# Weight tiles moved in pairs, 8 KB in a row for each partition, with twelve ring slots in place of ten and half the descriptor scratch

## The chip, the cores and the metric

The kernel runs on one core of one Trainium2 chip. The metric is the device time of one execution in microseconds, given as the median of several. Five engines work side by side: TensorE (PE; matrix products), VectorE (DVE), ScalarE (ACT), GpSimd (POOL) and SyncE (SP), which here only issues transfers. The core's 16 DMA engines serve the transfers of all of them. Everything is float32 except the one-hot factors.

## The reference

A two-layer decoder trunk over 272 tokens (16 meta tokens and 256 real ones) of width 1024. Layer 0 mixes tokens by latent attention, layer 1 by a gated linear recurrence; each is followed by the same kind of expert layer, which is what matters here:

```python
q = (xb @ w_query).reshape(-1, PEER_HEADS, 2, PEER_QHALF)
s = jnp.einsum('thpd,pkd->thpk', q, sub_keys)
sv, si = lax.top_k(s, PEER_TOPK)
...
eidx = jnp.take_along_axis(cidx, top_p, axis=-1)   # 16 experts of 16384 for each token and head
g = jax.nn.softmax(top_s, axis=-1)
act = jax.nn.gelu(jnp.einsum('thkd,td->thk', u_tab[eidx], xb))
return jnp.einsum('thk,thkd->td', g * act, v_tab[eidx])
```

So every token meets 128 experts (8 heads of 16), each one row of 4 KB in `u_tab` and one in `v_tab`, tables of 16384 rows (64 MB each per layer).

## The kernel before, in words

**The stream of tiles.** All weights pass through one ring in on-chip memory, `raw`, of `SLOTS` = 10 slots of 128 partitions by 4 KB (512 KB). `tiles_in_order` lists the 593 tiles of the whole program: 25 of the attention layer, 272 of the expert layer (16 query tiles, 128 of `u`, 128 of `v`), 24 of the recurrence, and 272 again. `Tiles.fetch` (L227 to L232), run by SyncE, issues one transfer for each tile; tile g waits until TensorE has finished tile g - 10 (the semaphore `done` counts two halves for each tile). TensorE waits for `landed` of the slot (L254) in `multiply_raw` (L259 to L271) for query and u tiles and in `apply_v` (L1161 to L1167) for v tiles. `fetch` of one stage reaches `SLOTS` tiles into the next, ahead of that stage's own small loads. `wait_halves` lets other engines wait for a place in the stream.

**The expert layer.** Its tokens are treated in two ways. For 160 of them (TD) the layer is computed densely: TensorE multiplies each u tile with all 160 tokens, ScalarE applies gelu (L1225) into `act_w`, VectorE multiplies in the gates, and TensorE applies each v tile to the result, collecting in PSUM. A float32 product appears as two matmul records, so a tile of 8 products is 16 records at L267 (queries, u) or L1159 (v). The gates are spread out by products of one-hot factors that VectorE builds in groups of 8 tokens (L1135 to L1142): 20 groups for each half of the experts, TensorE's part at L1122, 24 records for each group; they stand between the last 40 u tiles and between the first 40 v tiles, one for each two tiles. Before them TensorE waits, after u tile 84, for VectorE's `placed` (its products are at L1477).

The other tokens (112 in layer 0, 96 in layer 1) are done by gathering. GpSimd (L1179 to L1186) issues one indirect transfer for each set of 128 rows of 4 KB (512 KB, as much as a tile), into one of `NBUF` = 8 buffers: 112 of `u_rows` and then 112 of `v_rows` in layer 0, 96 and 96 in layer 1, 416 in all. It waits for the indices (`rows_found`) and for VectorE to have taken the row set 8 places earlier (`rows_taken`). VectorE takes a set of u rows with a product and sum (`dot`, L1316 to L1323) and a set of v rows with a multiply and add (`add_row`, L1330 to L1340). Where it does so is written out by hand: 6 sets after each pair of searches for the top 16 (L1357), 9 and 9 about the spreading of the gates (L1370, L1383), 2 with each group of one-hot factors (L1396), and the rest, 78 sets in layer 0 and 56 in layer 1, one by one, paced by the v tiles from 40 to 118 (L1400 to L1404).

**The end of the layer.** Before v tiles 112, 116, 120 and 124 (112, 116 and 124 in layer 1) TensorE folds in one copy of the gathered sums (L1492 to L1505, 16 records at L1501). Fold b waits until `rows_taken` has 32 (b + 1) sets of v rows; the last one waits for all of them.

**Memory.** The kernel's tensors nearly fill the on-chip memory; a part at its start, 16 KB for each partition by default, is kept for the descriptors of GpSimd's transfers (L1681).

Of the kernel before, what the change touches and what calls it, by code (L numbers as in the profile page):

```python
# [20 lines left out]
P = 128  # L21
D = 1024
DC = D // P
# [12 lines left out]
PH, NK, TOPK, QH = 8, 128, 16, 128  # L36
# [1 line left out]
HALF = NK // 2  # L38
ST = 8
PARTS = 3  # L40
SLOTS = 10
LEAD = 2
HW = D // 2

# [56 lines left out]
class Steps:  # L101


    def __init__(self, eng, sem):
        self.eng, self.sem, self.n = eng, sem, 0
# [109 lines left out]
class Tiles:  # L215

    def __init__(self, ctx, mem, tiles):
        self.mem, self.tiles = mem, tiles
        self.landed = [ctx.sem(f"landed{k}") for k in range(SLOTS)]
        self.done = ctx.sem("tiles_done")

    def fetch(self, sp, first, last):  # L227

        for g in range(first, min(last, len(self.tiles))):
            if g >= SLOTS:  # L230
                sp.wait_ge(self.done, 2 * (g - SLOTS + 1))
            sp.dma_start(self.mem.raw[:, g % SLOTS, :], self.tiles[g]).then_inc(self.landed[g % SLOTS], 16)  # L232


class Stream:
# [14 lines left out]
            pe.sem_inc(free, 1)  # L250

    def wait_landed(self, pe, n):
        g = self.base + n
        pe.wait_ge(self.mem.tiles.landed[g % SLOTS], 16 * (g // SLOTS + 1))  # L254

    def tile(self, n):
        return self.mem.raw[:, (self.base + n) % SLOTS, :]

    def multiply_raw(self, pe, n, out, x, scaled=None):  # L259

# [1292 lines left out]
def tiles_in_order(d):  # L1553

    def layer(n):
        v_tiles = d[f"v_rows{n}"].rearrange("(i p) f -> i p f", p=P)
        return ([d["query"][n][k] for k in range(2 * PH)] + [d["u"][n][k] for k in range(NK)]
                + [v_tiles[k] for k in range(NK)])

    mixed = [[d["mla_down"][k] for k in range(MLA_TILES - DC)] + [d["mla_out"][k] for k in range(DC)],  # L1560
             [d["lru_w"][k] for k in range(LRU_TILES)]]
    return mixed[0] + layer(0) + mixed[1] + layer(1)


# [62 lines left out]
def lay_out(inputs):  # L1627

    a = {k: np.asarray(v) for k, v in inputs.items()}
    chunked = lambda t: np.ascontiguousarray(t.T.reshape(DC, P, -1).transpose(1, 0, 2))  # L1630
    columns = lambda v: v.reshape(-1, P).T
    half = ROPE // 2
    swap = np.r_[half:ROPE, 0:half]

    w_in = a["mla_w_in"][0]
    lat, kr = w_in[:, :QLORA + KVLORA], w_in[:, QLORA + KVLORA:]
    q_up = a["mla_w_q_up"][0].reshape(QLORA, HEADS, NOPE + ROPE)
    q_rope = q_up[:, :, NOPE:]
    q_up = np.concatenate([x.reshape(QLORA, -1) for x in (q_rope, q_rope[:, :, swap], q_up[:, :, :NOPE])], axis=1)
    kv_up = a["mla_w_kv_up"][0].reshape(KVLORA, HEADS, NOPE + VH)  # L1640

    def half_tiles(w):
        w = w.reshape(-1, P, w.shape[1] // P, P).transpose(2, 0, 1, 3).reshape(-1, 4, P, P)
        return w.transpose(0, 2, 1, 3).reshape(-1, P, HW)

    k_up, v_up = kv_up[:, :, :NOPE].reshape(KVLORA, -1), kv_up[:, :, NOPE:].reshape(KVC, P, 2, HW)
    up = np.concatenate([half_tiles(q_up), half_tiles(k_up), v_up.transpose(2, 0, 1, 3).reshape(-1, P, HW)])
    up = up.reshape(-1, 2, P, HW).transpose(0, 2, 1, 3).reshape(-1, P, D)
    down = column_tiles(np.concatenate([lat, kr, kr, kr[:, swap], kr[:, swap]], axis=1))
    vec = [a["mixer_norm"][0], a["mixer_norm"][1], a["ffn_norm"][0], a["ffn_norm"][1], a["final_norm"],  # L1650
           a["lru_b_gate_a"][0], a["lru_b_gate_x"][0], a["lru_conv_b"][0], *a["lru_conv_w"][0], a["lru_lambda"][0],
           a["mla_q_norm"][0], a["mla_kv_norm"][0]]
    con, idm = constants()
    layers = a["peer_u"].shape[0]
    lru_in = a["lru_w_in"][0]
    u = a["peer_u"].reshape(layers, NK, NK, DC, P).transpose(0, 1, 4, 3, 2)
    return {
        "x": chunked(a["x"][0]),
        "meta": chunked(a["meta_tokens"]),
        "pos": np.ascontiguousarray(a["positions"]),  # L1660
        "con": con,
        "idm": idm,
        "vec": np.ascontiguousarray(np.concatenate([columns(v) for v in vec], axis=1)),
        "mla_down": np.concatenate([down, up]),
        "mla_out": column_tiles(a["mla_w_out"][0]),
        "query": column_tiles(a["peer_w_query"]),
        "keys": np.ascontiguousarray(a["peer_sub_keys"].transpose(0, 3, 1, 2)),
        "u": np.ascontiguousarray(u).reshape(layers, NK, P, D),
        **{f"u_rows{n}": np.ascontiguousarray(a["peer_u"][n]) for n in range(layers)},
        **{f"v_rows{n}": np.ascontiguousarray(a["peer_v"][n]) for n in range(layers)},  # L1670
        "lru_w": np.concatenate([column_tiles(w) for w in (lru_in[:, D:], lru_in[:, :D], a["lru_w_out"][0])]),
        "lru_wa": np.ascontiguousarray(a["lru_w_gate_a"][0].transpose(1, 0, 2)),
        "lru_wx": np.ascontiguousarray(a["lru_w_gate_x"][0].transpose(1, 0, 2)),
    }
# [16 lines left out]
```

## Time and profile before

| | |
|---|---|
| median of 3 runs | 1613.38 us (1613.03 to 1615.23) |
| the profiled execution | 1615.82 us |
| its span in the trace | 1613.8 us |
| TensorE busy | 1582.1 us (98%) |
| VectorE busy | 1101.5 us (68%) |
| GpSimd busy | 494.1 us (31%) |
| moved by DMA | 534.94 MB, mean 331 GB/s |
| SyncE's queue, packets and share of the 16 DMA engines | 89938, 50.7% |
| GpSimd's queue | 59904, 34.5% |

The rows below come from the trace of the profiled execution; their times count from the start of its span. A share of DMA above 1.00 means that packets of an engine overlap. In the list of stretches each engine's busy time stands with its number of instructions in brackets; in the chain and in the instruction lists a row begins with its start and its length. "<-" names what ended the idle time before an instruction.

### The profile page before, as it was taken

To read this page: it belongs to the slowest core of one execution; us is meant where nothing else is said; L and a number is where in the kernel's file an instruction comes from. 1 tells how busy PE (TensorE), PEld (TensorE's weight loads), DVE (VectorE), ACT (ScalarE), POOL (GpSimd) and SP (SyncE) were. 2 spreads that over 40 slices of the span, in tenths; PEclk is the share of its full clock that TensorE was granted. 3 is DMA by queue.
4 is the path that set the end of the run, shared out by engine and by line. 5 is a ranking of instruction groups with operands and counts; after the bars stand their busy time and mean duration, and the time that the engine had idled before them with its cause. 6 is when DMAs were issued, how large, how long until landed. Compare 5 with 4: busy or idle time off the path is not lost.

```text
span 1613.8 us, 30119 instructions
## 1 busy us (share of the span) xinstructions
PE 1582.1 (98%) x12128; PEld 1506.9 (93%) x12128; DVE 1101.5 (68%) x2478; ACT 209.5 (13%) x604; POOL 494.1 (31%) x423
## 2 busy tenths in 40 slices
PE   9999999999899999999999999999999999999997
PEld 7688899999899999998898888999999999999997
DVE  3373379998899998545537425999879989944441
ACT  2251221111011000000003312111211100000000
POOL 0000033335444456533300001333534435533310
PEclk9999999999999999999999999999999999999999
DMA  6304489999999999999984446999999999999991
GB/s 245 131 16 147 137 304 389 384 394 406 409 408 409 401 409 408 409 409 409 409 326 155 144 149 227 339 397 386 396 409 408 408 405 408 408 410 408 409 378 60
DMA packets 149979, 534.94 MB, mean 331 GB/s; under 512 B 17617, under 2 KB 20434, under 8 KB 149842
## 3 DMA queue, kind: packets, MB, share of 16 engines
q1 hardware_dynamic: 89938, 314.90, 50.7%
q0 software_dynamic: 59904, 218.13, 34.5%
q8 instruction: 96, 1.57, 0.4%
q14 instruction: 41, 0.34, 0.1%
HBM read 531.92 MB, written 1.05 MB: 330 GB/s over the span
## 4 chain that ended last, share of the span: by engine, by line
PE 79%; DVE 10%; DMA 8%; issue 3%; ACT 0%; DVEq 0%; SPq 0%; ACTq 0%; POOLq 0%
PE ps L267 37%; PE ps L1159 30%; DMA raw<-in_v_rows 6%; PE ps L1122 4%; DVE big L1322 3%; PE ps L728 2%; PE ps L279 2%; DMA big<-in_u_rows,big 2%; DVE big L1272 1%; PE ps L1501 1%; PE ps L738 1%; DVE big L1268 1%; PE ps L1433 1%; DVE big L1298 1%; DVE big L1300 1%
## 5 line engine op out<-in xcount | busy, mean ns | idle before, releaser
L267 PE MATMUL ps<-big,raw 128*128 128x160 f32 (+2 forms) x5104 | 798.5, 318 | 2.5 <-ACT big L1225 2.5
L267 PEld LDWEIGHTS ps<-big,raw 128*128 128x128 f32 x5104 | 751.5, 191 | 35.6 <-issue 3.1
L1159 PE MATMUL ps<-big,raw 128*128 128x160 f32 x4096 | 579.1, 301 | 6.5 <-DVE big L1154 2.3
L1159 PEld LDWEIGHTS ps<-big,raw 128*128 128x128 f32 x4096 | 559.6, 190 | 15.7 <-DMA raw<-in_v_rows 12.7
L1185 POOL DMA_INDIRECT big<-in_u_rows,big x208 | 250.3, 1203 | 733.4 <-DVE big L1308 376.5
L1339 DVE SCALAR_TENSOR_TENSOR big<-big 128x1024 f32<-128x1024 f32 x201 | 258.0, 1284 | 191.3 <-PE ps L1159 107.7
L1185 POOL DMA_INDIRECT big<-in_v_rows,big x208 | 240.5, 1156 | 320.6 <-DVE big L1339 255.1
L1322 DVE CUSTOM_DVE_ANT_0 big<-big 128x1024 f32<-128x1024 f32 x208 | 244.4, 1222 | 22.4 <-DMA big<-in_u_rows,big 19.8
L1225 ACT ACTIVATE big<-ps 128x160 f32<-128x160 f32 x256 | 77.4, 303 | 512.7 <-PE ps L267 474.0
L374 ACT ACTIVATE big<-h 128x272 f32<-128x272 f32 (+1 forms) x32 | 12.7, 419 | 645.8 <-DVE h L1414 597.3
L1268 DVE MAX8 big<-big 128x8 f32<-128x128 f32 (+1 forms) x99 | 33.5, 339 | 88.3 <-ACT big L1194 76.3
L1142 DVE TENSOR_TENSOR i_gate<-i_hot,g 128x512 bf16<-128x512 bf16 x240 | 87.2, 419 | 0.0
L1122 PEld LDWEIGHTS ps<-i_gate,j_hot 128*128 128x128 bf16 x1920 | 69.3, 98 | 7.9 <-DVE i_gate L1142 4.9
L1122 PE MATMUL ps<-i_gate,j_hot 128*128 128x64 bf16 x1920 | 71.6, 193 | 4.6 <-DVE i_gate L1142 4.6
L1154 DVE TENSOR_TENSOR big<-big,ps 128x512 f32<-128x512 f32 x80 | 54.8, 685 | 24.5 <-PE ps L1122 21.4
L1138 DVE TENSOR_TENSOR j_hot<-iota,idx 128x1024 bf16<-128x1024 bf16 x80 | 54.8, 685 | 0.0
L789 DVE TENSOR_TENSOR h<-h,ps 128x272 f32<-128x272 f32 (+1 forms) x16 | 6.9, 429 | 44.2 <-PE ps L267 44.2
L1135 DVE TENSOR_TENSOR i_hot<-iota,idx 128x512 bf16<-128x512 bf16 x80 | 33.5, 419 | 0.1
L279 PE MATMUL ps<-big,raw 128*128 128x272 f32 (+1 forms) x128 | 30.3, 390 | 2.4 <-DVE big L577 2.4
L1272 DVE FIND_INDEX8 big<-big 128x8 uint32<-128x128 f32 (+1 forms) x99 | 31.1, 333 | 0.0
L1271 DVE FIND_INDEX8 big<-big 128x8 uint32<-128x128 f32 (+1 forms) x99 | 31.1, 332 | 0.0
L279 PEld LDWEIGHTS ps<-big,raw 128*128 128x128 f32 x128 | 24.2, 190 | 7.2 <-DMA raw<-in_mla_down 2.7
(173 smaller groups left out, 762.7 us busy)
## 6 DMA issues: line engine op xcount, KB each, us to landing
raw<-in_u SPq DMA_DIRECT2D x256, 512.0 KB
raw<-in_v_rows SPq DMA_DIRECT2D x256, 512.0 KB
raw<-in_query SPq DMA_DIRECT2D x32, 512.0 KB
raw<-in_lru_w SPq DMA_DIRECT2D x24, 512.0 KB
raw<-in_mla_down SPq DMA_DIRECT2D x17, 512.0 KB
raw<-in_mla_out SPq DMA_DIRECT2D x8, 512.0 KB
big<-in_u_rows,big POOLq DMA_INDIRECT x208
big<-in_v_rows,big POOLq DMA_INDIRECT x208
```

Of the source, the lines that this page charges most:

```text
L267: mm = pe.matmul(out, w[:, c * P:(c + 1) * P], x[:, c, :], start=(c == 0), stop=(c == DC - 1))
L279: mm = pe.matmul(self.bank(n), self.tile(n)[:, c * P:(c + 1) * P], x[:, c, :], start=(c == 0), stop=(c == DC - 1), skip_group_check=True)
L1122: mm = pe.matmul(o, mem.j_hot[:, t // 2, :, t % 2], mem.i_gate[:, k, t // 2, :, t % 2], start=(k == 0), stop=(k == PARTS - 1))
L1138: step.add(dve.tensor_tensor(mem.j_hot[:, :, :, :], mem.iota[:, :, :].unsqueeze(1).to_broadcast(wide), pairs(mem.idx[:, 1, tok], wide), AL ...
L1142: ins = dve.tensor_tensor(mem.i_gate[:, k], mem.i_hot[:, :, :, :], pairs(mem.g[:, k, tok], wide_i), ALU.mult)
L1154: dve.tensor_tensor(w, w, g, ALU.mult).then_inc(gated, 1)
L1159: return pe.matmul(accumulator(c), w, act_w[:, i, :], start=start, stop=False, skip_group_check=True)
L1185: pool.indirect_dma_start(bufs[:, b, :], None, (u_rows if n < ROWS else v_rows)[:, :], bass.IndirectOffsetOnAxis(rows_at[:, k:k + 1], 0)). ...
L1225: act.activation(act_w[:, i:i + 1, :], mem.ps[:, i % 2, 0:TD].unsqueeze(1), ACT.Gelu_apprx_tanh).then_inc(st.free[i % 2], 1)
L1268: for k, op in enumerate((lambda v, spare, f, at: dve.max(f[:, 0:8], v), lambda v, spare, f, at: dve.match_replace(spare, f[:, 0:8], v, NE ...
L1322: dve.tensor_tensor_reduce(buf, buf, reps[:, copy_of(n), :], 1.0, 0.0, ALU.mult, ALU.add, dots[:, n:n + 1]).then_inc(rows_taken, 1)
L1339: dve.scalar_tensor_tensor(rep, bufs[:, n % NBUF, :], w, rep, ALU.mult, ALU.add).then_inc(rows_taken, 1)
```

## The change

Query, u and v tiles are laid out in device memory in pairs, so that each partition's part of two tiles lies in 8 KB on end, and one transfer moves both into two neighbouring slots. The tiles of attention and recurrence stay single. The ring has 12 slots. A transfer is issued once both its slots are free. The v tiles now come from an array of their own, laid out in pairs, and no longer from the one that the gathers read. The scratch for the descriptors of GpSimd's transfers goes from 16 KB to 8 KB for each partition.

```diff
-SLOTS = 10
+SLOTS = 12
...
-    def __init__(self, ctx, mem, tiles):
-        self.mem, self.tiles = mem, tiles
+    def __init__(self, ctx, mem, transfers):
+        self.mem, self.transfers = mem, transfers
         self.landed = [ctx.sem(f"landed{k}") for k in range(SLOTS)]
         self.done = ctx.sem("tiles_done")
+        self.sem_of, self.count, self.total, used = [], [], 0, [0] * SLOTS
+        for count, _ in transfers:
+            k = self.slot(self.total)
+            assert k + count <= SLOTS
+            used[k] = used[k] + 16
+            self.sem_of = self.sem_of + [self.landed[k]] * count
+            self.count = self.count + [used[k]] * count
+            self.total = self.total + count
+
+    def slot(self, g):
+        return (g + 1) % SLOTS
+
+    def wait_landed(self, pe, g):
+        pe.wait_ge(self.sem_of[g], self.count[g])
 
     def fetch(self, sp, first, last):
 
-        for g in range(first, min(last, len(self.tiles))):
-            if g >= SLOTS:
-                sp.wait_ge(self.done, 2 * (g - SLOTS + 1))
-            sp.dma_start(self.mem.raw[:, g % SLOTS, :], self.tiles[g]).then_inc(self.landed[g % SLOTS], 16)
+        g = 0
+        for count, tiles in self.transfers:
+            if first <= g < last:
+                k = self.slot(g)
+                if g + count > SLOTS:
+                    sp.wait_ge(self.done, 2 * (g + count - SLOTS))
+                sp.dma_start(self.mem.raw[:, k:k + count, :], tiles).then_inc(self.landed[k], 16)
+            g = g + count
...
     def layer(n):
-        v_tiles = d[f"v_rows{n}"].rearrange("(i p) f -> i p f", p=P)
-        return ([d["query"][n][k] for k in range(2 * PH)] + [d["u"][n][k] for k in range(NK)]
-                + [v_tiles[k] for k in range(NK)])
+        return ([(2, d["query"][n][k]) for k in range(PH)] + [(2, d["u"][n][k]) for k in range(NK // 2)]
+                + [(2, d["v"][n][k]) for k in range(NK // 2)])
...
+    def by_two(tiles):
+        tiles = tiles.reshape(layers, -1, 2, P, D).transpose(0, 1, 3, 2, 4)
+        return np.ascontiguousarray(tiles)
...
-        "query": column_tiles(a["peer_w_query"]),
+        "query": by_two(column_tiles(a["peer_w_query"])),
...
-        "u": np.ascontiguousarray(u).reshape(layers, NK, P, D),
+        "u": by_two(u),
+        "v": by_two(a["peer_v"]),
...
-    nc = bacc.Bacc("TRN2", target_bir_lowering=False, num_devices=1)
+    nc = bacc.Bacc("TRN2", target_bir_lowering=False, num_devices=1, dynamic_dma_scratch_size=8192)
```

## Rows read from the trace of the kernel before

**Rows 1.** The page: TensorE, the packets, and the two queues that carry nearly all.
```profile
PE 1582.1 (98%) x12128; PEld 1506.9 (93%) x12128; DVE 1101.5 (68%) x2478; ACT 209.5 (13%) x604; POOL 494.1 (31%) x423
...
DMA packets 149979, 534.94 MB, mean 331 GB/s; under 512 B 17617, under 2 KB 20434, under 8 KB 149842
...
q1 hardware_dynamic: 89938, 314.90, 50.7%
q0 software_dynamic: 59904, 218.13, 34.5%
```

**Rows 2.** Busy time by stretches; last columns: TensorE's clock, DMA share, GB/s.
```profile
0.00:25.00 25.00, 21.21 (x101) 16.53 (x102) 11.52 (x33) 6.62 (x9) 3.27 (x7) 1.00 0.87 315
...
375.00:825.00 450.00, 436.13 (x3883) 425.39 (x3882) 332.12 (x507) 20.14 (x61) 201.53 (x173) 0.99 1.03 408
...
600.00:625.00 25.00, 25.00 (x276) 24.81 (x276) 24.48 (x39) 0.00 (x0) 12.94 (x10) 1.00 1.03 408
...
700.00:725.00 25.00, 24.31 (x169) 22.84 (x168) 11.37 (x10) 0.00 (x0) 8.43 (x9) 1.00 1.03 409
725.00:750.00 25.00, 23.77 (x158) 21.35 (x157) 12.55 (x10) 0.00 (x0) 9.37 (x10) 1.00 1.03 409
750.00:775.00 25.00, 23.82 (x158) 21.40 (x157) 12.26 (x11) 0.00 (x0) 9.33 (x10) 1.00 1.03 409
775.00:800.00 25.00, 23.85 (x162) 21.68 (x160) 12.11 (x10) 0.00 (x0) 8.86 (x10) 1.00 1.03 409
...
1404.00:1560.00 156.00, 156.00 (x1158) 156.00 (x1154) 67.43 (x54) 0.00 (x0) 49.10 (x50) 1.00 1.03 409
```

**Rows 3.** The chain of waits in order of time, v tiles of layer 0; end of layer 1.
```profile
629.46 69.64 PE ps L1159 x512
...
774.03 23.17 DMA raw<-in_v_rows
797.24 2.44 PE ps L1159 x16
799.68 1.70 PE ps L1501 x16
...
820.64 1.70 PE ps L1501 x16
...
831.12 1.69 PE ps L1501 x16
...
1590.52 1.70 PE ps L1501 x16
```

**Rows 4.** VectorE's instructions in order of time, rows of V taken in layer 0.
```profile
660.57 1.28 DVE L1339 SCALAR_TENSOR_TENSOR big<-big 128x1024 f32<-128x1024 f32 x1 [1.26 <-DMA big<-in_v_rows,big]
663.13 1.28 DVE L1339 SCALAR_TENSOR_TENSOR big<-big 128x1024 f32<-128x1024 f32 x1 [1.28 <-DMA big<-in_v_rows,big]
...
823.18 1.28 DVE L1339 SCALAR_TENSOR_TENSOR big<-big 128x1024 f32<-128x1024 f32 x1 [1.27 <-DMA big<-in_v_rows,big]
```

**Rows 5.** VectorE and TensorE in order of time, before the one-hot products of layer 0.
```profile
419.59 1.23 DVE L1322 CUSTOM_DVE_ANT_0 big<-big 128x1024 f32<-128x1024 f32 x1 [1.32 <-DMA big<-in_u_rows,big]
...
404.93 1.41 PE L1477 MATMUL ps<-token,big 128*128 128x16 bf16 x50 [1.20 <-DVE big L1379]
...
424.11 1.46 PE L1122 MATMUL ps<-i_gate,j_hot 128*128 128x64 bf16 x24 [4.63 <-DVE i_gate L1142]
```

**Rows 6.** The same of layer 1, and the last row that it takes.
```profile
1191.25 1.23 DVE L1322 CUSTOM_DVE_ANT_0 big<-big 128x1024 f32<-128x1024 f32 x1 [1.33 <-DMA big<-in_u_rows,big]
...
1194.63 1.09 DVE L1142 TENSOR_TENSOR i_gate<-i_hot,g 128x512 bf16<-128x512 bf16 x3
...
1201.30 0.89 PE L1122 MATMUL ps<-i_gate,j_hot 128*128 128x64 bf16 x24
...
1571.39 1.28 DVE L1339 SCALAR_TENSOR_TENSOR big<-big 128x1024 f32<-128x1024 f32 x1 [0.89 <-PE ps L1159]
```

**Rows 7.** GpSimd's gathers of V: nanoseconds of one (shortest, median, longest).
```profile
L1185 POOL DMA_INDIRECT big<-in_v_rows,big x208: 932/940/1876, 524.7 to 1547.8; - x104
```

More of the change, by code:

```diff
@@ L252, in wait_landed @@
     def wait_landed(self, pe, n):
-        g = self.base + n
-        pe.wait_ge(self.mem.tiles.landed[g % SLOTS], 16 * (g // SLOTS + 1))
+        self.mem.tiles.wait_landed(pe, self.base + n)
     def tile(self, n):
-        return self.mem.raw[:, (self.base + n) % SLOTS, :]
+        return self.mem.raw[:, self.mem.tiles.slot(self.base + n), :]
     def multiply_raw(self, pe, n, out, x, scaled=None):
@@ L1555, in layer, with single @@
     def layer(n):
-        v_tiles = d[f"v_rows{n}"].rearrange("(i p) f -> i p f", p=P)
-        return ([d["query"][n][k] for k in range(2 * PH)] + [d["u"][n][k] for k in range(NK)]
-                + [v_tiles[k] for k in range(NK)])
-    mixed = [[d["mla_down"][k] for k in range(MLA_TILES - DC)] + [d["mla_out"][k] for k in range(DC)],
-             [d["lru_w"][k] for k in range(LRU_TILES)]]
+        return ([(2, d["query"][n][k]) for k in range(PH)] + [(2, d["u"][n][k]) for k in range(NK // 2)]
+                + [(2, d["v"][n][k]) for k in range(NK // 2)])
+    def single(tile):
+        return 1, tile.unsqueeze(1)
+    mixed = [[single(d["mla_down"][k]) for k in range(MLA_TILES - DC)] + [single(d["mla_out"][k]) for k in range(DC)],
+             [single(d["lru_w"][k]) for k in range(LRU_TILES)]]
     return mixed[0] + layer(0) + mixed[1] + layer(1)
@@ L1655, in lay_out @@
     lru_in = a["lru_w_in"][0]
-    u = a["peer_u"].reshape(layers, NK, NK, DC, P).transpose(0, 1, 4, 3, 2)
+    u = a["peer_u"].reshape(layers, NK, NK, DC, P).transpose(0, 1, 4, 3, 2).reshape(layers, NK, P, D)
+    def by_two(tiles):
+        tiles = tiles.reshape(layers, -1, 2, P, D).transpose(0, 1, 3, 2, 4)
+        return np.ascontiguousarray(tiles)
     return {
```

## The prediction

> **What bounds the kernel now.** I read the page first, then the busy time by stretches, then the chain of waits, then the instruction lists of the two expert stages. The page shows TensorE busy for 98% of the span, and two DMA queues sharing the 16 DMA engines: SyncE's, which streams the 512 KB tiles, and GpSimd's, which gathers 512 KB of table rows at a time; together about 85% of the engines' time [rows 1]. The stretches show where the second number matters. From 375 to 825 us, in layer 0, the engines are full: share 1.03, 408 GB/s [rows 2]. So one 512 KB transfer costs 524,288 B / 409 GB/s = 1.28 us of the DMA engines, whichever queue it is from, and in this stretch any transfer that comes earlier pushes another one back by 1.28 us.
>
> TensorE needs less than that. From 629.46 us 512 matmul records, 32 tiles of 16 records, take 69.64 us: 2.176 us a tile [rows 3], or 241 GB/s. But with both queues loaded each gets every other turn: the vector engine's row steps come 2.56 us apart behind the gathers [rows 4], exactly 2 x 1.28, which leaves the tile stream one tile in 2.56 us too. TensorE eats the tiles that had been fetched ahead, and from about 700 us starves. Four stretches of 25 us hold 169, 158, 158 and 162 records where 25 / 2.176 x 16 = 184 would fit [rows 2]; the chain of waits has the tile transfers in it there, the last until 797.24 us [rows 3]. The missing 89 records are 12 us.
>
> The end of the stage is set by a second condition. Before V tiles 112, 116, 120 and 124 TensorE folds in the gathered rows (the 16-record pieces at 799.68, 820.64 and 831.12), each fold waiting for 32 more rows to be taken, the last one for all 224. The last row had landed at 823.18 and was taken at 824.46 [rows 4]; the last fold began at 831.12 [rows 3]. So today the gathers end 6.7 us before they are needed, and the tiles are what is late. Both draw on the same DMA time: the tiles are late, the gathers have 6.7 us in hand.
>
> **The change part by part.** *Rows of 8 KB in each transfer.* Both queues now move 4 KB rows: nearly all packets lie between 2 and 8 KB, and the 593 tile transfers are 144 packets each, as are the 416 gathers [rows 1]. Equal packets and equal shares: that fits engines which take a packet from each queue in turn. It would fit turns by bytes as well, and the trace can't tell the two apart. I take turns by packet. The tile queue then moves 8 KB for each 4 KB of a gather and can have 2/3 of 409 = 273 GB/s, above the 241 it needs. The ring of tiles stays full and TensorE doesn't starve.
>
> The Trainium skill ("DMA: Bandwidth & Descriptors", "Queues, rings and completion order") says that each DMA engine goes round its queues a packet at a time. By that rule it is the change of packet that moves the shares, and the rule speaks against this change; with turns by bytes in its place the result is the first rival's.
>
> Gain for TensorE: from 629.46, 72 tiles up to V tile 112 at 2.176 us are 156.7, so fold 0 at 786.1 in place of 799.7; then 10.48 us for each fold with its four tiles (831.12 - 820.64), so it stands before fold 3 at 817.6 in place of 831.1: 13.5 us sooner [rows 3].
>
> Price for the gathers: what is fetched sooner for TensorE is taken from them, and the last gather is found by counting transfers. Tile 111 had landed by 797.24 [rows 3], and at one in 2.56 us ten more by 823.2: 122 V tiles. After the change TensorE is held before tile 124 with a full ring, and twelve slots mean that tiles 124 to 135 (the last eight already those of the recurrent layer) have landed: 136. These 14 extra transfers come before the last gather: 14 x 1.28 = 17.9 us, so it lands at 841.1, is taken 1.3 us later, and fold 3 begins at 842.4, **11.3 us later** than now. The 13.5 us are gained and then waited away: TensorE stands idle some 25 us at folds 2 and 3. Nothing gives that back: the full ring goes into a stage that is not short of DMA.
>
> *Rate of the longer rows.* No row shows 8 KB packets. Lowest end: no gain, since at a share of 1.03 the packets already overlap. Highest end: the first 25 us, where part of the packets are 1 KB, move 315 GB/s at share 0.87, or 362 at share 1, against 409/1.03 = 397 later: 10% [rows 2]. I take 2%, near the low end, as the engines are never without a packet in the stretch that counts. From 375 us to the last gather about 183 tiles land (47 u tiles and 136 of V), so 1% is 183 x 1.28 x 0.01 = 2.3 us, and 2% is 4.7. Fold 3 at 837.7: **+6.6 us**.
>
> The Trainium skill ("Perfetto Trace Analysis", "DMA Optimizations") holds that going from 2 KB to 4 or 8 KB can raise throughput dramatically; the runs so far show nothing from 4 to 8. Its page "DMA: Bandwidth & Descriptors" ("Bandwidth") gives 425 GB/s for a 16 MB transfer; as an estimate that would be 4%, and the sum +2.
>
> *The earlier join in layer 0.* At 380 to 424 us TensorE waits 1.2 us for `placed` and 4.63 us for the first one-hot products, behind rows that land every 2.56 us [rows 5]. With the ring kept full, gathers get 409 - 241 = 168 GB/s, 3.1 us each, while TensorE runs, and all of it while it stands. In those 38 us TensorE takes about 16.3 tiles against 15 landed, so the gathers are set back by 1 to 2 transfers: 0 to 2.5 us. This is inside the 14 counted above, as the DMA engines are full from here to the last gather; alone it would not set the end.
>
> *The stretch with one-hot products* (424 to 629): two tiles and two rows in each 5.15 us are 407 GB/s, and VectorE is busy 24.48 of 25 us [rows 2]. The gathers keep 409 - 204 = 205 GB/s, just their need. Costs nothing, but has no margin.
>
> *Layer 1.* The rows taken just before the products come from the gather of 1191.25, the products begin at 1201.30 [rows 6]: VectorE has the first one-hot tiles ready at 1195.7, which leaves 5.6 us of cover, and the setback there is about 2 to 3 transfers, 2.6 to 3.8 us. The last row is taken by 1572.7, fold 2 comes at 1590.5 [rows 3, 6]; even ten transfers more, 12.8 us, are covered. TensorE is busy 156.0 of 156 us from 1404 to 1560 [rows 2], so nothing is gained either: 0. If that cover were gone, each transfer would cost 1.28.
>
> *Two more slots, pairs, fewer issues.* A pair is issued when both its slots are free and is usable when both tiles are in, but at 12 slots it is asked for no later than 10 tiles ahead of use, which is what a tile has now. SyncE issues half as many transfers; it mostly waits. 0.
>
> *Half the scratch.* A gather is 144 packets on 16 engines, 9 on each, and at most 8 are under way: 72 entries. GpSimd takes 0.94 us for one [rows 7] against 2.56 between them, so even a wait of a microsecond at each wrap hides. Between 0 and 1 us; 0.
>
> Sum: +6.6 us. The profiled execution took 1615.82 us (span 1613.8), 2.4 above the median of 1613.38: 1622.4 in its terms, **1620.0** in those of the median.
>
> **Rivals.** *Shares stay equal* (turns by bytes). For it: the trace fits it as well. The tiles keep one turn in two; two more slots are worth at most 2 x 2.56 = 5.1 us where they could be filled before the drought, and 2% on some 158 tiles gives 4.0. Between 0 and 9 us sooner, the 6.7 us that the gathers have in hand being nearly the cap; taken 4: 1609.4. Chance 0.23.
>
> *The rate decides: faster.* Shares shift, but 8 KB rows run over 4.8% faster; there 4.8 x 2.3 us cancel the 11.3. At 8% fold 3 comes at 842.4 - 18.7 = 823.7, 7.4 sooner: 1606.0; TensorE's own arrival caps it at 13.5. Against it: the share of 1.03. Chance 0.12.
>
> *The change doesn't do what it says*: the hardware cuts 8 KB rows into 4 KB packets again. Then only the slots count: 0 to 5 us sooner, taken 2.5: 1610.9. Chance 0.10.
>
> Forecast: 0.55. Its own range is 1613 (4.6% more rate) to 1627 (no gain, and two tiles miscounted: 11.3 + 2.6).
>
> **Numbers.** The range takes in the first and third rival and the forecast, and leaves out the larger gains of the rate: 1608.0 to 1627.0. A measurement here tells about 0.2%, 3.2 us, from nothing. Faster by more: 0.15 of the first rival, 0.10 of the second, 0.04 of the third: 0.29. Within: 0.16. Slower: 0.55.
>
> **What would show it.** Right: SyncE's queue falls from 89,938 to about 50,800 packets; 700 to 800 us hold some 736 records in place of 647 and no tile transfer stands in the chain; rows there come about 3.1 us apart; TensorE waits at L1501 for VectorE's L1339 some 15 to 25 us in all, and the last fold of layer 0 begins near 838. Wrong: rows still 2.56 us apart (equal shares), over 420 GB/s in the full stretch (the rate), or the last fold before 831.

## The result, and the profile of the changed kernel

Four executions of the changed kernel took 1628.67 us in the median (1625.92 to 1630.10), four of the kernel before 1614.31 (1613.03 to 1615.55). The ratio is **1.0087**, 95% interval 1.0070 to 1.0104: slower by 14 us, where 6.6 was forecast. The profiled execution took 1630.1 us, its span is 1628.0, 14.2 longer than before.

The page of the changed kernel, beside [rows 1]:

```profile
PE 1578.0 (97%) x12128; PEld 1510.6 (93%) x12128; DVE 1102.1 (68%) x2478; ACT 209.5 (13%) x604; POOL 495.4 (30%) x423
...
DMA packets 110810, 534.91 MB, mean 329 GB/s; under 512 B 13266, under 2 KB 16083, under 8 KB 75859
...
q1 hardware_dynamic: 50770, 314.89, 48.9%
q0 software_dynamic: 59904, 218.13, 34.1%
```

SyncE's queue has 39,168 packets fewer. That is 272 pairs x 144: a pair is now 144 packets, as one tile was, 9 on each of the 16 engines. And 4,351 of the packets under 512 B are gone, 16 for each of the 272 pairs (4,352) but for one. So a transfer's ninth packet on each engine is a small one beside eight rows. This will matter below.

Its stretches, with the columns of [rows 2] (last three: TensorE's clock, DMA share, GB/s):

```profile
375.00:825.00 450.00, 432.41 (x3923) 429.77 (x3921) 319.54 (x496) 20.20 (x61) 198.80 (x172) 0.98 1.02 410
600.00:625.00 25.00, 25.00 (x276) 24.81 (x276) 24.48 (x40) 0.00 (x0) 12.67 (x11) 1.00 1.02 406
700.00:725.00 25.00, 25.00 (x186) 25.00 (x185) 10.29 (x9) 0.00 (x0) 7.48 (x8) 1.00 1.02 414
725.00:750.00 25.00, 25.00 (x186) 25.00 (x185) 10.28 (x8) 0.00 (x0) 8.42 (x9) 1.00 1.02 417
...
775.00:800.00 25.00, 25.00 (x192) 25.00 (x191) 12.03 (x10) 0.00 (x0) 10.27 (x10) 1.00 1.02 415
800.00:825.00 25.00, 18.15 (x137) 17.90 (x135) 11.11 (x10) 0.00 (x0) 9.11 (x10) 0.92 1.02 410
825.00:850.00 25.00, 11.92 (x65) 11.79 (x65) 13.77 (x17) 0.58 (x2) 2.29 (x2) 0.60 0.43 159
1404.00:1560.00 156.00, 156.00 (x1205) 155.88 (x1204) 74.98 (x72) 0.00 (x0) 54.91 (x54) 1.00 1.02 415
```

TensorE no longer starves from 700 to 800 us: 186 and 192 records in 25 us where there were 158 to 169. The engines move 415 GB/s there in place of 409. Then comes the price. From 825 to 850 us TensorE works for less than half of the time, at a granted clock of 0.60 (0.50, the lower of its two levels, from 838 to 842 us), while the DMA engines are at 0.43: the ring is full, the last gathers land, and everything waits for VectorE and for one fold. The chain of waits, in order of time, beside [rows 3]:

```profile
785.45 19.62 DMA big<-in_v_rows,big
805.15 1.30 DVE big L1352
...
809.17 17.57 DMA big<-in_v_rows,big
826.82 1.30 DVE big L1352
...
836.74 1.29 DVE big L1352
838.08 3.59 PE ps L1514 x16
841.67 8.34 PE ps L1172 x48
...
1604.78 1.71 PE ps L1514 x16
```

Gathers stand where tiles stood. The fold that began at 831.12 [rows 3] begins at 838.08, and takes 3.59 us where it took 1.69; the 48 records after it take 8.34. In the kernel before the same chain read:

```profile
832.81 6.62 PE ps L1159 x48
...
846.34 6.42 PE ps L279 x28
```

The rows of V that VectorE takes, in order of time, beside [rows 4]; 34 of them between 699.26 and 798.80 us are 3.02 us apart in the mean:

```profile
666.26 1.29 DVE L1352 SCALAR_TENSOR_TENSOR big<-big 128x1024 f32<-128x1024 f32 x1 [0.92 <-DMA big<-in_v_rows,big]
669.41 1.28 DVE L1352 SCALAR_TENSOR_TENSOR big<-big 128x1024 f32<-128x1024 f32 x1 [1.86 <-PE ps L1172]
...
826.82 11.20 DVE L1352 SCALAR_TENSOR_TENSOR big<-big 128x1024 f32<-128x1024 f32 x8 [0.32 <-DMA big<-in_v_rows,big]
```

The last eight come back to back, 1.4 us each: once the ring is full, gathers land at least as fast as VectorE takes them. TensorE in order of time (the last fold, then the two joins), and VectorE's last late row of u in layer 1, beside [rows 5, 6]:

```profile
838.08 3.59 PE L1514 MATMUL ps<-con,big 128*128 128x16 f32 x16 [19.93 <-DVE big L1352]
...
424.86 1.46 PE L1135 MATMUL ps<-i_gate,j_hot 128*128 128x64 bf16 x24 [6.99 <-DVE i_gate L1155]
...
1197.01 1.40 PE L1490 MATMUL ps<-token,big 128*128 128x16 bf16 x50
...
1214.22 1.46 PE L1135 MATMUL ps<-i_gate,j_hot 128*128 128x64 bf16 x24 [2.67 <-DVE i_gate L1155]
...
1209.70 1.23 DVE L1335 CUSTOM_DVE_ANT_0 big<-big 128x1024 f32<-128x1024 f32 x1 [2.21 <-DMA big<-in_u_rows,big]
```

**The ledger of the 14.2 us.** The last fold of layer 0 begins 7.0 us later. The fold and the 48 records behind it take 3.59 + 8.34 in place of 1.69 + 6.62, so 3.6 us go to the clock. Layer 1 loses about 4: there TensorE has a new wait of 2.67 us for the one-hot products and starts them at half clock (1.46 us for 24 records where [rows 6] has 0.89). The sum is 14.6 less some tenths gained elsewhere; after the join nothing more is lost (1604.78 against 1590.52 at the last fold of layer 1 is +14.26). Single places move more than the sum does: the same kernel, executed again for experiment 6, has its last fold of layer 0 at 835.52, its new wait in layer 1 at 3.74 us and the last fold of layer 1 some 13.3 us later than before. So 2.5 us between two profiles at the last fold of layer 0 tell nothing by themselves.

### The profile page after: what moved, and what is told of

Its sections match the earlier page's. It is cut to its first block, busy times and chain, and to the rows that moved or that the text cites. A ratio compares the mean times of both kernels' runs of the same rounds, so it can differ in the third digit from the quotient of the medians.

```text
span 1628.0 us, 29847 instructions
## 1 busy us (share of the span) xinstructions
PE 1578.0 (97%) x12128; PEld 1510.6 (93%) x12128; DVE 1102.1 (68%) x2478; ACT 209.5 (13%) x604; POOL 495.4 (30%) x423
## 3 DMA queue, kind: packets, MB, share of 16 engines
q1 hardware_dynamic: 50770, 314.89, 48.9%
## 4 chain that ended last, share of the span: by engine, by line
PE 52%; DVE 25%; DMA 14%; issue 7%; POOL 1%; ACT 0%; DVEq 0%; another core or an unknown queue 0%; SPq 0%; POOLq 0%; ACTq 0%
PE ps L280 23%; PE ps L1172 18%; DMA big<-in_v_rows,big 10%; DVE big L1335 7%; DMA big<-in_u_rows,big 4%; DVE big L1352 4%; PE ps L1135 3%; PE ps L741 2%; PE ps L292 2%; DVE i_gate L1155 2%; DVE big L1285 1%; DVE big L1281 1%; DVE big L1311 1%; DVE big L1313 1%; DVE big L1167 1%
## 5 line engine op out<-in xcount | busy, mean ns | idle before, releaser
L280 PEld LDWEIGHTS ps<-big,raw 128*128 128x128 f32 x5104 | 752.1, 191 | 35.6 <-issue 3.0
L1172 PE MATMUL ps<-big,raw 128*128 128x160 f32 x4096 | 571.4, 301 | 2.2 <-DVE big L1167 2.2
L1172 PEld LDWEIGHTS ps<-big,raw 128*128 128x128 f32 x4096 | 560.5, 191 | 2.9 <-issue 2.4
L1352 DVE SCALAR_TENSOR_TENSOR big<-big 128x1024 f32<-128x1024 f32 x201 | 258.0, 1283 | 203.5 <-PE ps L1172 109.6
L1514 PE MATMUL ps<-con,big 128*128 128x32 f32 (+1 forms) x112 | 14.8, 286 | 19.9 <-DVE big L1352 19.9
L1514 PEld LDWEIGHTS ps<-con,big 128*128 128x128 f32 x112 | 14.8, 212 | 20.2 <-DVE big L1352 20.2
L1285 DVE FIND_INDEX8 big<-big 128x8 uint32<-128x128 f32 (+1 forms) x99 | 31.1, 330 | 0.0
```

Source lines behind the costliest of these rows:

```text
L280: mm = pe.matmul(out, w[:, c * P:(c + 1) * P], x[:, c, :], start=(c == 0), stop=(c == DC - 1))
L1172: return pe.matmul(accumulator(c), w, act_w[:, i, :], start=start, stop=False, skip_group_check=True)
L1352: dve.scalar_tensor_tensor(rep, bufs[:, n % NBUF, :], w, rep, ALU.mult, ALU.add).then_inc(rows_taken, 1)
```

## The experiments

Each ratio is against runs of the kernel before on the same chip; brackets hold the 95% interval. A thousandth is 1.6 us.

**1. Only the scratch halved.**

```diff
-    nc = bacc.Bacc("TRN2", target_bir_lowering=False, num_devices=1)
+    nc = bacc.Bacc("TRN2", target_bir_lowering=False, num_devices=1, dynamic_dma_scratch_size=8192)
```

> The kernel before with the descriptor scratch at 8 KB and nothing else. Theory (the longer packets of the tile queue take turns from the gathers): the scratch has no part, 1613 to 1616 us, rows still 2.56 us apart in layer 0, GpSimd's busy time within 5 us of 494. Rival (the smaller scratch makes GpSimd issue later): slower by 5 us or more, GpSimd's gaps put down to issue well above 83 us.

0.9999 [0.9989, 1.0008], last fold at 831.05. The scratch costs nothing, with single tiles at least.

**2. Only two more slots** (and the smaller scratch), tiles single: `SLOTS = 12` in the kernel before.

> The kernel before with twelve slots and the 8 KB scratch; tiles still single, 4 KB in a row. Theory: shares stay equal, two more tiles are in hand before the drought of layer 0, so it is 0 to 5 us faster than before, 1609 to 1615 us. Rival (the deeper ring alone sets the gathers back): the last fold of layer 0 begins later than 831 us and the time is above 1616.

0.9976 [0.9966, 0.9985]; on another chip again:

> Twelve slots and the 8 KB scratch with single tiles, again, beside the mixed kernel and in more rounds: 3 to 6 us below before (ratio 0.9976 the first time).

0.9975 [0.9963, 0.9987], 1609.90 us. TensorE stands before the last fold at 824.91 us and waits for nothing:

```profile
824.91 1.85 PE L1501 MATMUL ps<-con,big 128*128 128x16 f32 x16
```

It gains 6 us there (5 in the repeat, which has the fold at 825.91) and 4 in all. This version beats both kernels. It is the change without its pairs.

**3. The change with its 8 KB rows cut to 4 KB**: a pair is still one transfer.

```diff
-                sp.dma_start(self.mem.raw[:, k:k + count, :], tiles).then_inc(self.landed[k], 16)
+                sp.dma_start(self.mem.raw[:, k:k + count, :], tiles, max_dma_last_dim=4 * D).then_inc(self.landed[k], 16)
```

> The changed kernel in all but one thing: each 8 KB row of a pair is cut into two pieces of 4 KB, so the layout, the pairs, the twelve slots and the scratch are those of the change and only the packets are as before. Theory: the packet's size does it, so rows in layer 0 are 2.56 us apart again, the DMA rate falls from 416 to 409 GB/s, no fold waits for rows, and the time is 1609 to 1615 us. Rival (pairs that land together, or the ring, or the layout do it): it stays near 1628.

1.0021 [1.0011, 1.0031]. The expectation was missed: the last fold still waits for rows, 4.52 us in place of 19.93, and begins at 830.08:

```profile
830.08 2.86 PE L1514 MATMUL ps<-con,big 128*128 128x16 f32 x16 [4.52 <-DVE big L1352]
```

The 8 KB rows are the larger part of the loss: 1.0087 against 1.0021 is 10.7 us, with the repeat below up to 13. But against experiment 2 there are also 7 us between single tiles and pairs, packets of 4 KB in both, which the forecast had at nothing. Experiments 9 to 12 are about these.

**4. The change with ten slots** in place of twelve.

> The changed kernel with ten slots in place of twelve, 8 KB rows kept. Theory: the tile stream still has priority, and when TensorE stands at the last fold of layer 0 two tiles fewer have been fetched ahead of the last rows, so the fold begins about 2.5 us sooner (near 835.5) and the time is 2 to 4 us below the change, about 1625.5. Rival (the ring's depth does most): 8 us or more below the change.

1.0097 [1.0080, 1.0115]: the time is that of the change, and the 2 to 4 us expected are not there. The last fold is at 836.21, near the 835.5 expected, but the unaltered change has 838.08 and 835.52 in two profiles, so that shows nothing. The profiled span is 1627.7, the wait at the join of layer 1 is 3.14 in place of 2.67. No worth of the extra slots is to be seen once the rows are 8 KB.

**5. Turn by packet, from the other side**: the kernel before with the tiles' rows cut to 2 KB, one execution.

```diff
-            sp.dma_start(self.mem.raw[:, g % SLOTS, :], self.tiles[g]).then_inc(self.landed[g % SLOTS], 16)
+            sp.dma_start(self.mem.raw[:, g % SLOTS, :], self.tiles[g], max_dma_last_dim=2 * D).then_inc(self.landed[g % SLOTS], 16)
```

> The kernel before with each tile's 4 KB rows cut into 2 KB pieces, gathers left at 4 KB. Theory (the engines take a packet from each queue in turn): where both queues are loaded the gathers get 2/3, so VectorE no longer waits for rows of V in layer 0, the last row is there well before the fold, TensorE starves earlier and longer, and the time is some microseconds above before. Rival (turns by bytes): rows stay 2.56 us apart and the waits stay as before, but for what the smaller packets cost in rate.

1649.47 us beside 1616.87, where "some microseconds" were expected. Waits of this kernel (engine, line, what it waited for: us in total, times, longest):

```profile
DVE big L1339 <- PE ps L1159: 194.5, 122, 4.1
PEld ps L1159 <- DMA raw<-in_v_rows: 37.1, 51, 1.6
PE ps L1159 <- DMA raw<-in_v_rows: 24.7, 45, 1.3
```

VectorE no longer waits for a gathered row of V at all (79.6 us in the kernel before); it waits for TensorE, and TensorE for tiles. Equal bytes per turn would have left these waits as they were, but for a rate of 397 GB/s in place of 408. So shorter rows on the tile queue favour the gathers, as turns by packet would have it. The size of the shift isn't seen here: VectorE takes most rows of V one for each v tile, so the gathers can't run away, and from 700 to 800 us 607 records passed where there were 640, the tiles still having about half of the bytes. The full two thirds that were expected for the gathers were not reached. How exact the turns are is shown by experiments 3, 10 and 12. The Trainium skill ("DMA: Bandwidth & Descriptors", "Queues, rings and completion order") states that the engines change queues at packets, and of the direction the trace agrees. It puts some 9 to 17 descriptors in a packet, though, and the counts below come out only with each row as a turn of its own; there the measurement decides.

**6. The clock**: 150, then 190 products of a constant before the last fold's wait, so that TensorE isn't idle in it.

```diff
+                if layer == 0 and b == COPIES - 1:
+                    keep_busy(pe, mem, GBANK, 150)
```

> The changed kernel with 150 small products on constant data ahead of TensorE's last fold of layer 0, where it stands idle for 20 us and its granted clock then falls to 0.60 of the stretch. They fill the wait and change nothing else. Theory: part of the 14 us is the clock after the idle time; the fold takes 1.7 to 1.9 us in place of 3.6 and the next 48 records 6.6 in place of 8.3, the time is 3 to 4 us below the change (ratio to before about 1.0065 against 1.0087). Rival (the clock's fall costs nothing on the path): the same as the change.

> The changed kernel with 190 small products ahead of the last fold of layer 0 in place of 150, which left 3.4 us of the wait open and the fold at 3.0 us. Theory (a low granted clock after the wait costs 3 to 4 us): with the wait filled the fold takes 1.9 us, the next 48 records 6.6 us, and the time is 2 to 4 us below the change. Rival: the clock's part is under 1 us and the same as the change is measured again.

With 150 the products ended 3.44 us before the fold; the fold took 3.00 us, the next 48 records 9.05: the clock had fallen all the same, to 0.50 from 841 to 843 us, and the time was that of the change, 1.0081 [1.0060, 1.0102]. With 190 the gap was gone (TensorE in order of time):

```profile
814.18 20.91 PE L212 MATMUL ps<-filler 128*128 128x256 bf16 x190
834.92 1.86 PE L1516 MATMUL ps<-con,big 128*128 128x16 f32 x16
836.62 6.77 PE L1172 MATMUL ps<-big,raw 128*128 128x160 f32 x48
```

Fold and records are back at their old lengths, the granted clock from 825 to 850 us is 1.00 in place of 0.60, and the time is 1625.81, 1.0076 [1.0060, 1.0092]. The change itself, in the same series:

> The change as it is, on the chip of the three kernels beside it, so that they are compared with it directly. 12 to 16 us above before, last fold of layer 0 at 836 to 840 us.

1630.39, 1.0102 [1.0078, 1.0126]. TensorE in order of time:

```profile
835.52 3.59 PE L1514 MATMUL ps<-con,big 128*128 128x16 f32 x16 [20.11 <-DVE big L1352]
```

So idle time at the fold costs about 3.6 us beyond itself by the records. The two spans are 3.1 us apart and the two medians 4.6, but of four executions each, with intervals that overlap: the records are the firmer evidence.

**7. Hold back the tiles of the next stage** until the last row of layer 0 is taken.

```diff
-        mem.tiles.fetch(sp, st.base + SLOTS, st.base + PEER_TILES + SLOTS)
+        mem.tiles.fetch(sp, st.base + SLOTS, st.base + PEER_TILES)
+        if layer == 0:
+            sp.wait_ge(rows_taken, 2 * ROWS)
+        mem.tiles.fetch(sp, st.base + PEER_TILES, st.base + PEER_TILES + SLOTS)
```

> The changed kernel, but the tiles of the recurrent layer are not asked for before the last row of layer 0 has been taken; TensorE can't use them earlier. Theory (each tile that is fetched ahead of the last gathers costs them one transfer): 8 transfers less before the last row, so the last fold begins 8 to 10 us sooner, at 828 to 830 us, and the time is 8 to 12 us below the change, 1617 to 1621. Rival (the gathers' delay comes from elsewhere, such as how their transfers are served beside long packets): less than 4 us gained.

1.0010 [0.9996, 1.0024]. VectorE and TensorE in order of time:

```profile
809.28 21.13 DVE L1355 SCALAR_TENSOR_TENSOR big<-big 128x1024 f32<-128x1024 f32 x15 [0.51 <-DMA big<-in_v_rows,big]
```
```profile
830.47 3.59 PE L1517 MATMUL ps<-con,big 128*128 128x16 f32 x16 [10.44 <-DVE big L1355]
```

Fifteen rows are now back to back: without the tiles fetched ahead into the recurrent layer, gathers land at least as fast as VectorE takes them, and the fold is 7.6 us earlier than in the change, 5.1 earlier than in its repeat. By the ratios the gain is 12 to 15 us; the profiled execution (1623.09, the median is 1617.72) shows only 7 of them. The ten times fall in two groups, six from 1615.2 to 1617.9 and four from 1621.7 to 1623.8, with the profiled one in the upper; what parts them no trace shows.

**8. Only the u tiles' rows cut to 4 KB.**

```diff
+                at = (g - MLA_TILES) % (PEER_TILES + LRU_TILES)
+                row = 4 * D if 2 * PH <= at < 2 * PH + NK else 8 * D
+                sp.dma_start(self.mem.raw[:, k:k + count, :], tiles, max_dma_last_dim=row).then_inc(self.landed[k], 16)
```

> The changed kernel with the rows of the u tiles cut to 4 KB, query and v tiles as in the change. Theory (the join of layer 1 stalls because rows of u come later beside long packets): TensorE doesn't wait for the first one-hot products of layer 1, which saves the 4 us by which the change stretches that part, and the last fold of layer 0 moves little; 3 to 5 us below the change. Rival (all the loss sits at the last fold of layer 0): within 1 us of the change.

1.0060 [1.0044, 1.0077]. The wait at the join of layer 1 is gone (the products begin at 1212.63, 0.89 us for 24 records), while the last fold of layer 0 is where it was (837.67, after 19.41 us). The two losses are separate: of the 14 us some 3 (by the spans, 1625.1 for 1628.0) to 4 (by the ratios) belong to the u tiles.

**9. Single tiles, asked for by two**: twelve slots, but each two tiles are requested when both slots are free, and land by themselves.

```diff
+            at = (g - MLA_TILES) % (PEER_TILES + LRU_TILES)
+            ahead = 1 if g >= MLA_TILES and at < PEER_TILES and at % 2 == 0 else 0
...
-                sp.wait_ge(self.done, 2 * (g - SLOTS + 1))
+                sp.wait_ge(self.done, 2 * (g - SLOTS + 1 + ahead))
```

> Twelve slots with single tiles of 4 KB rows, as in the kernel with twelve slots, but in the expert layers two tiles are asked for at the same moment, when the second one's slot is free, as a pair is; each still has its own transfer and its own semaphore. Theory (pairs cost because TensorE can't use the first tile of a pair before the second has landed): like twelve slots with single tiles, ratio 0.9975 within 0.001. Rival (pairs cost because they are asked for later and in lumps): near the kernel with pairs cut to 4 KB, ratio 1.001 to 1.003.

0.9981 [0.9972, 0.9990], as good as experiment 2 within the intervals. Asking later is not what pairs cost. The last fold comes at

```profile
826.34 1.96 PE L1503 MATMUL ps<-con,big 128*128 128x16 f32 x16
```

**10. Pairs in 4 KB rows, with the hold** of experiment 7.

> Pairs with their rows cut to 4 KB, twelve slots, and the recurrent layer's tiles held back until the last row of layer 0 is taken. Theory (with pairs more tiles lie ahead of the last gathers, and the 4.5 us wait at the last fold and the clock after it are the price): the wait for rows there goes, the last fold begins near 826 us and the ratio falls from 1.0021 to 0.997 to 0.999. Rival (the price of pairs is in TensorE's waits for tiles): the ratio stays above 1.001.

1.0020 [1.0011, 1.0029], last fold at 830.41 after 6.63 us, where 826 was expected: the hold does nothing here. The expectation was missed, so the gathers were not late through the filling of the ring. They were late all along. VectorE's rows in experiment 3, in order of time:

```profile
709.30 1.28 DVE L1352 SCALAR_TENSOR_TENSOR big<-big 128x1024 f32<-128x1024 f32 x1 [1.27 <-DMA big<-in_v_rows,big]
712.01 1.28 DVE L1352 SCALAR_TENSOR_TENSOR big<-big 128x1024 f32<-128x1024 f32 x1 [1.43 <-DMA big<-in_v_rows,big]
714.58 1.29 DVE L1352 SCALAR_TENSOR_TENSOR big<-big 128x1024 f32<-128x1024 f32 x1 [1.28 <-DMA big<-in_v_rows,big]
717.29 1.28 DVE L1352 SCALAR_TENSOR_TENSOR big<-big 128x1024 f32<-128x1024 f32 x1 [1.43 <-DMA big<-in_v_rows,big]
```

By turns 2.57 and 2.71 us, 2.64 in the mean, where single tiles give 2.56 each time. A count of packets explains it. A pair sent as one transfer has its 16 rows on each engine and one small packet, 17; two single tiles have 18. While a gather takes its 9 turns, SyncE's queue takes 9 too: one single tile, or 9/17 of a pair, which is 1.059 tiles. Then a row costs (1 + 1.059) x 1.28 = 2.64 us. SyncE's queue in experiment 3 has 85,586 packets, 4,352 = 272 x 16 under the 89,938 of [rows 1].

**11 and 12. Joint landing, or the packet saved?** Both keep 4 KB rows and the joint landing, and bring back the 18 packets. First by halves of the partitions:

```diff
+                part = P // count
+                for h in range(count):
+                    rows = slice(h * part, (h + 1) * part)
+                    sp.dma_start(self.mem.raw[rows, k:k + count, :], tiles[rows], max_dma_last_dim=4 * D).then_inc(self.landed[k], 16)
```

> The kernel with pairs in rows cut to 4 KB, each pair moved by two transfers, one for partitions 0 to 63 and one for 64 to 127, both of both tiles: the two tiles still become usable together, but a pair is now 2 x 9 = 18 packets on each engine (its 16 rows and two packets that announce the end) in place of 17, as two single tiles are. Theory A (the packets are counted, 18 turns against 17): the queue of tiles had 18/17 of its fair share, (2 + 1/17) x 1.28 = 2.64 us for a row against 2.56, which is the 3% that the rows of the pairs ran behind; now SyncE's queue has 89,938 packets again, rows are 2.56 us apart from 700 to 820, the last row of layer 0 is taken near 822.5, no wait at the last fold, and the time is that of single tiles asked for by two, 0.998 of before. Theory B (landing together is what costs): rows 2.63 apart as before this edit, the last fold near 830 after a wait of 4 to 7 us, 1.002 of before.

1.3568 [1.3527, 1.3608], 2189.88 us. This told nothing of the question: with 64 partitions in a transfer the full engines moved (stretch, columns as above)

```profile
375.00:825.00 450.00, 342.65 (x2962) 332.56 (x2962) 251.48 (x472) 29.05 (x86) 120.53 (x110) 0.92 1.03 272
```

272 GB/s where [rows 2] has 408. So by tile, both on one semaphore that TensorE awaits for either:

```diff
+                for h in range(count):
+                    sp.dma_start(self.mem.raw[:, k + h, :], tiles[:, h, :]).then_inc(self.landed[k], 16)
```

> As the kernel with pairs in rows cut to 4 KB, but each pair is moved by two transfers of one whole tile each (128 partitions), both counted on one semaphore that TensorE awaits for both: the tiles still become usable together, and a pair is 2 x 9 = 18 packets on each engine in place of 17. The split by halves of the partitions was no test of this: its engines moved 265 GB/s in place of 409. Theory A (the packets are counted, 18 turns against 17): SyncE's queue has 89,938 packets, rows are 2.56 us apart from 700 to 820 in place of 2.63, the last row of layer 0 is taken near 822.5, the last fold has no wait for it or one under 1 us, and the time is about that of single tiles asked for by two, 0.998 of before. Theory B (landing together is what costs): rows 2.63 apart, the last fold near 830 after a wait of 4 to 7 us, 1.002 of before.

1.0002 [0.9993, 1.0011]: between the two theories. VectorE's last rows and TensorE, in order of time:

```profile
818.86 1.28 DVE L1353 SCALAR_TENSOR_TENSOR big<-big 128x1024 f32<-128x1024 f32 x1 [1.27 <-DMA big<-in_v_rows,big]
821.41 1.29 DVE L1353 SCALAR_TENSOR_TENSOR big<-big 128x1024 f32<-128x1024 f32 x1 [1.27 <-DMA big<-in_v_rows,big]
823.97 1.28 DVE L1353 SCALAR_TENSOR_TENSOR big<-big 128x1024 f32<-128x1024 f32 x1 [1.27 <-DMA big<-in_v_rows,big]
```
```profile
784.60 4.61 PE L1173 MATMUL ps<-big,raw 128*128 128x160 f32 x32 [0.47 <-DMA raw<-in_v]
789.72 4.61 PE L1173 MATMUL ps<-big,raw 128*128 128x160 f32 x32 [0.51 <-DMA raw<-in_v]
...
830.74 1.85 PE L1515 MATMUL ps<-con,big 128*128 128x16 f32 x16
```

The rows are 2.56 us apart again, so the packet saved is what had slowed them: that theory is right about the gathers. But the fold isn't at 825. TensorE comes to it at 830.74, after one wait of half a microsecond for each pair, since with 18 packets the tiles have their old half and can only be used when the second is in. Joint landing costs TensorE 4.4 us at the fold (830.74 against 826.34 in experiment 9). In this step the layout in pairs and the v tiles' own array come in too; both versions move 409 GB/s from 700 to 800 us, and the waits stand once for each pair, so the landing is the likely cause, but the layout was not tried alone. Saving a packet gives the tiles back what it takes from the gathers. Both versions reach the fold at 830 to 831. The one with 17 packets stands idle 4.52 us ahead of it and loses the clock as well (2.86 + 9.20 us against 1.85 + 6.77), 3.4 us, enough for the whole of 1.0021 against 1.0002.

**13. A mixture**: query and u tiles single, v tiles in pairs of 8 KB, the hold, and 80 constant products before the last fold.

> Query and u tiles single with 4 KB in a row, v tiles in pairs with 8 KB, twelve slots, the 8 KB scratch, the recurrent layer's tiles held back until the last row of layer 0 is taken, 80 small products ahead of the last fold. Theory: no stall more than before at the join of layer 1, 8 transfers less ahead of the last rows, no drought of tiles, little loss by the clock: last fold at 825 to 829 us, the time 2 to 6 us below before, near the kernel with twelve slots alone. Rival (the gathers of v come too late beside long packets whatever is held back): above before.

0.9999 [0.9990, 1.0008]. The fold begins at 827.92, after a wait of 2.17 us, and takes 3.60. It mends what the change costs, but the 2 to 6 us expected below the kernel before are not there, and it is no match for single tiles in twelve slots.

## Why the prediction was partly wrong

**The parts, by ratio:**

| version | ratio | step, us |
|---|---|---|
| scratch halved | 0.9999 | 0 |
| two more slots | 0.9976 | -4 |
| asked for by two | 0.9981 | +1 |
| usable only by two | 1.0002 | +3 |
| one transfer, 17 packets for 18 | 1.0021 | +3 |
| rows of 8 KB (the change) | 1.0087 | +11 |

The versions were timed on different chips, each beside the kernel before, and a step of 1 is within its intervals.

The direction and the mechanism were right, the size was not: +14 in place of +6.6, 1628.67 against 1620.0, above the range's 1627.0.

*The join of layer 0: right.* TensorE's wait there grew from 4.63 to 6.99 us, the products begin 0.75 us later (0.4 sooner in the repeat), and it lies inside the setback of the last fold.

*Turns by packet: right.* 50,770 packets for 50,800; 744 records from 700 to 800 us for 736; no tile transfer in the chain; rows 3.0 us apart for 3.1; TensorE waiting 19.9 us for L1352 (L1339 before) where 15 to 25 were named. Experiment 3 shows that the rows' size is what moves the shares, experiment 5 that it works the other way too, though not by how much; the first rival falls by the records and the rows' distance, the third by the packets.

*The last fold: right*, 838.08 for 837.7, and 835.52 in the repeat. The transfers fetched ahead are a large part of what costs it: experiment 7, which holds back the eight of the next stage, worth 10.2 us by the count, gets 7.6 us back (5.1 against the repeat). To 0.4 us it is luck: the two profiles are 2.6 apart, the rate term was too large (below), and the count left out that the last eight rows are paced by VectorE.

*Rate: right in size, not in reach.* From 700 to 800 us 415 GB/s (414 to 417) against 409 is 1.5%, for 2% taken; 4 KB against 2 KB is 409 against 397, 3%. The second rival falls. But the sum took the 2% for all tiles from 375 us on, 4.7 us. From 375 to 825 us the engines moved 410 GB/s for 408, which as an estimate is 0.9 MB more, or 2.2 us (413 GB/s in the repeat, some 5). The Trainium skill ("Perfetto Trace Analysis", "DMA Optimizations") says that batching small transfers, of 2 KB into 4 or 8 KB for example, can raise throughput dramatically; with rows of these lengths inside transfers of 512 KB and more, these runs show 3% and 1.5%.

*The step that failed, first: the idle time at the last fold was priced at its length alone.* "Nothing gives that back" was right, but the clock adds to it. The forecast had TensorE idle some 20 to 25 us before the last folds and priced only the wait: its sum has no term for the clock. After the wait the granted clock is at half, and 64 records cost 3.6 us more. Experiment 6 shows it: with 150 products and 3.44 us idle the clock still fell, with 190 and no gap it stayed at full and the records had their old lengths.

*Second: the cover at the join of layer 1.* "the setback there is about 2 to 3 transfers, 2.6 to 3.8 us", under 5.6 us of cover. TensorE entered the stretch 10.1 us later than before (1197.01 for 1186.92), and the last row came 18.45 us later (1209.70 for 1191.25): a setback of 8.4 us. Of 8.4 us the cover of 5.6 leaves 2.8, and the wait is 2.67; with the half clock after it the layer loses about 4 us. Experiment 8 removes just this by giving the u tiles 4 KB rows. Why the setback is so large was only argued: for layer 0 the transfers had been counted over a window of fixed length, 38 us, but while the gathers are late TensorE goes on, eats tiles, and each one puts them back by another transfer. With n transfers at the start that is, as an estimate, x = 1.28 x (n + x / 2.176), 6.2 us for 2 and 9.3 for 3. No experiment varied it.

*Third: two more slots, pairs and fewer issues at 0.* With rows of 4 KB neither is 0: two slots gain 4 us, pairs cost 6 to 7. In the 14 us of the change no part of it can be pointed out: its ledger closes without one, and with rows of 8 KB two slots less changed nothing (experiment 4). The sentence that a pair is "asked for no later than 10 tiles ahead of use" looked at when it is asked for, which indeed costs nothing (experiment 9), and not at when its first tile is usable nor at how many packets it is.

What stays open: why experiment 7's times fall in two groups, its median 5 us below its profiled execution; what the layout in pairs does by itself; and whether the setback in layer 1 grows as the estimate has it.

## What to carry to other kernels

When two queues fill the DMA engines, count each transfer's packets, the small one at its end too: shares go by turns, so longer rows on one queue are taken from the other, and a merged transfer is also a later first tile. Before feeding the engine that starves, ask how many microseconds the other queue has in hand (here 6.7), and count its setback over all the time in which the consumer runs on. A wait that appears at TensorE can cost some microseconds more than its length.

## What the runs showed of the hardware

- Packet turns are exact enough to calculate with: 18 packets against 9 and 9 give 2.56 us for a row, 17 give 2.64 by the count and 2.57 and 2.71 by turns in the trace.
- Transfers over 64 of the 128 partitions, on the same number of packets, moved 272 GB/s in place of 408, gathers included, and the kernel took a third longer.
- TensorE's clock fell after short waits too. After 2.17 us idle (behind 80 constant products) the last fold of layer 0 took 3.60 us in place of 1.86, after 3.44 us 3.00, after 4.52 us 2.86, after 10 and 20 us 3.59. With the 48 records behind it the cost was 3.3 to 4.3 us in all of them, so it hardly depends on the length of the wait. But the clock doesn't fall after every short wait. Behind the two waits below, of experiment 7 in layer 1 and experiment 9 in layer 0, the granted clock was 1.00 for the next 7 us and the 24 records kept their 0.90 us. The length of a wait alone doesn't tell here whether the clock will fall.

```profile
1208.38 0.90 PE L1135 MATMUL ps<-i_gate,j_hot 128*128 128x64 bf16 x24 [2.29 <-DVE i_gate L1155]
423.52 0.90 PE L1124 MATMUL ps<-i_gate,j_hot 128*128 128x64 bf16 x24 [3.06 <-DVE i_gate L1144]
```

- With the tile queue held back, gathered rows land at least every 1.4 us, where VectorE becomes their bound (15 rows in 21.13 us).
